# Output projection of a decoder layer: two column chunks at once, with two of eight row tile pairs by Strassen's scheme

## The chip, the core and the metric

One core of a Trainium2 chip runs one layer of a decoder trunk in float32. The metric is the device time in microseconds (us) of one execution. Engines: TensorE (PE) multiplies matrices into PSUM; VectorE (DVE) and ScalarE (ACT) work elementwise; GpSimd (POOL) does a little; SyncE (SP) issues nearly all transfers.

## The reference

The step around the change is the third line; all the others stay as they are.

```python
y_a = multiscale_pool(u_pool, pool_mix_w[i], pool_scale[i]) @ w_branch_a[i]
y_b = hgrn2(q, f_logit, inp, g, lb_all[i], hgrn_norm_w[i]) @ w_branch_b[i]
merged = jax.nn.sigmoid(gate_a) * y_a + jax.nn.sigmoid(gate_b) * y_b
x = x + merged @ w_out[i]                 # (256, 2048) @ (2048, 2048)
h2 = rms_norm(x, ln_ffn_w[i])
u = causal_depthwise_conv(h2 @ w_up[i], conv_w[i], conv_b[i])
```

There are 256 tokens and a model width of 2048.

## The kernel before

**Precision.** TensorE multiplies a shortened float32 form, so every operand is split into a high part and a remainder (hi and lo). One product of blocks is a triple of matmuls (`triple`, L717; the same in `row_tile`, L654): hi by hi, hi by lo, lo by hi. Each matmul has a 128x128 block of tokens as the stationary operand and 128x512 weights as the moving one.

**Units.** All weights are streamed through a ring of RING = 4 buffers. A unit is one transfer of two row tiles (2 x 128 rows) of 512 columns, 512 KB, into `raw`. ScalarE copies it to `w_hi` (`split_hi`, L1108), VectorE writes the remainder `w_lo` (`split_lo`, L1411), and TensorE multiplies it with the two row tiles of both token blocks: 2 x 2 triples, 12 matmuls (`unit`, L665). Units are numbered through the kernel: the mixer's gates and branches from MIX, the output projection from WOUT, the up projection from UP, the down projection from DOWN. A transfer into a buffer waits until the unit four before is split (`slot_split`, L481).

**Slots.** ScalarE and VectorE work through slots with a handwritten order, `slot(s)` (L1277 and L1756). Slot s first splits unit s + 3 (LEAD = 3); ScalarE's split waits until TensorE is through with unit s - 1, so slot s runs beside TensorE's unit s. Then follow the other steps that are due at s, in the order in which they stand in the code. An engine that waits holds all that stands behind it in its queue.

**The output projection before.** WOUT = UP - 32. Four column chunks of 512 one after the other, eight units each. `chunk_unit` (L698) waits for a free accumulator (`main`, one of two), multiplies, and runs what is due on TensorE behind the unit: `turn_m` (L709, turns the last merged chunk, behind unit 2) and `side` (L937). Chunk n ends at `out_slot(n)`. Then, for chunk n: VectorE adds the accumulator to x (L1838, two additions of 128x512, in slot out_slot(n)); TensorE turns x by eight transposes, `x1T` + n, behind unit out_slot(n) + 1, and waits for these additions before (L964); ScalarE squares x with a sum (L1166, slot + 1); ScalarE and VectorE write the high and low blocks of xT from the turned ones (L1143 and L1457, slot + 2). The up projection (L827) reads these blocks of xT; its first eight units are narrow (256 columns in all) and need a chunk of xT for every two of them.

**What already uses Strassen's scheme.** The gates of the mixer (chunks 1 to 3, both gates at a time, pairs GATES_AT = (2, 4)) and the down projection. For a pair of row tiles and two chunks, the 2 x 2 blocks of tokens and the 2 x 2 blocks of weights need 8 triples; the scheme needs 7, with sums of blocks. VectorE forms the differences of weights (`weight_diffs`, L1661) two slots ahead, ScalarE and VectorE split them in two halves (`sums_hi`, `sums_lo`); GpSimd and VectorE form the sums of the activations (`join_parts`, `act_sums`); TensorE does its part of them two units later (`gate_weight_sums`, L804). At the end the four products beside the accumulators are recombined by additions on VectorE (`combine_gates`, `combine`).

Of the kernel before, what the change touches and what calls it, by code (L numbers as in the profile page):

```python
# [36 lines left out]
P = 128  # L37
# [15 lines left out]
NCOL = 512  # L53
# [53 lines left out]

def out_slot(n):
    return WOUT + UK * (n + 1)
# [17 lines left out]
GATES_AT = (2, 4)  # L127
N_GATES = len(GATES_AT) * (NQ - 1)
SEVENS = [gate_unit(n, i) for n in range(1, NQ) for i in GATES_AT] + [down_unit(p, i) for p in range(2) for i in SEVEN_AT[p]]
SEVEN = {u: q for q, u in enumerate(SEVENS)}  # L130
ACT_SUMS = [0, 1] + SEVENS[N_GATES:]
SUMS_AT = {max(u - 4, DOWN + UK) if f > 1 else MIX + 2 * UK - 2 + 3 * f: f for f, u in enumerate(ACT_SUMS)}
N_SEVEN = [N_GATES + len(SEVEN_AT[0]), len(SEVENS)]
COMBINED0 = 4 * (NQ - 1)
# [67 lines left out]
GATES_COMBINE_AT = [gate_unit(n, GATES_AT[-1]) + 5 for n in range(NQ)]  # L202
COMBINE_AT = [down_slot(2 * p) - 4 for p in range(2)]
# [18 lines left out]
def build(nc, x, x_t, p_t, vecs, convs, w_in, pool_mix_w, w_branch_a, w_branch_b, w_out, w_up, w_down,  # L222
          w_ple_gate, w_ple, ln_final_w, ident_c, levels_c, counts_c, out):
    with ExitStack() as ctx:
# [255 lines left out]
        def _(sp):  # L480
# [70 lines left out]
            for n in range(NQ):  # L551
                for i in range(UK):
                    rows(u, w_out_v, 2 * i, n * NCOL)
                    x_tok_piece(u)
                    u += 1
# [46 lines left out]
        def _(pe):  # L602
# [123 lines left out]
            def act_sum(q, k):  # L726
                return a_sums_hi[:, q % 2, k, :], a_sums_lo[:, q % 2, k, :]
# [18 lines left out]
            def down_seven(u, p, i, a):  # L746

                q = SEVEN[u - a]
                first, end = i == SEVEN_AT[p][0], i == SEVEN_AT[p][-1]
                pe.wait_ge(lo_full, u + 1)  # L750
                if a == 0:
                    if first:
                        if p:
                            pe.wait_ge(xT_ready, 4 * (2 * NQ + 2))
                        else:
                            pe.wait_ge(z_read, NUP + 1)
                    triple(product(p, 0), *act_block(2 * i, 0), *ring_tile(u, 0), start=first, stop=end)
                    mm = triple(down_acc(2 * p, 0), *act_block(2 * i + 1, 0), *ring_tile(u, 1), start=False, stop=False)
                else:
                    pe.wait_ge(a_sums_ready, q + 3 - N_GATES)  # L760
                    mm = triple(down_acc(2 * p + 1, 0), *act_sum(q, 2), *ring_tile(u, 1), start=False, stop=False)
                mm.then_inc(units_done, 1)
# [26 lines left out]
            def gate_seven(u, n, i, a):  # L789

                q = SEVEN[u - a]
                first, end = i == GATES_AT[0], i == GATES_AT[-1]
                pe.wait_ge(lo_full, u + 1)
                if a == 0:
                    if first:
                        pe.wait_ge(gated, 4 * n)
                    triple(gate_product(0), *x_block_t(2 * i, 0), *ring_tile(u, 0), start=first, stop=end)
                    mm = triple(main[:, 0, 0, :], *x_block_t(2 * i + 1, 0), *ring_tile(u, 1), start=False, stop=False)
                else:
                    pe.wait_ge(a_sums_ready, q % 2 + 1)  # L800
                    mm = triple(main[:, 1, 0, :], *act_sum(q, 2), *ring_tile(u, 1), start=False, stop=False)
                mm.then_inc(units_done, 1)

            def gate_weight_sums(u, n, i, half):  # L804
# [9 lines left out]
                else:  # L814
                    triple(gate_product(2), *act_sum(q, 0), *sum_tile(q, 2), start=first, stop=end)
                    mm = triple(main[:, 0, 1, :], *x_block_t(2 * i + 1, 1), *sum_tile(q, 3), start=False, stop=False)
                mm.then_inc(w_sums_done, 1)
# [207 lines left out]
            for n in range(NQ):  # L1025
                for i in range(UK):
                    if n == 0 and i % 2 == 0:
# [79 lines left out]
        def _(ac):  # L1107
# [153 lines left out]
            def sums_hi(q, part):  # L1261

                if part == 0:
                    ac.wait_ge(a_summed, q + 1)
                    if q > 1:
                        ac.wait_ge(w_sums_done, 2 * (q + N_GATES - 3))
# [10 lines left out]
            def slot(s):  # L1277
# [23 lines left out]
                for p in range(2):  # L1301
                    if s == COMBINE_AT[p] - 1:
# [107 lines left out]
        def _(dve):  # L1410
# [317 lines left out]
            def combine(p, part):  # L1728

                c0, c1 = cols(2 * p), cols(2 * p + 1)  # L1730
                p5, p6, p7 = (product(p, k) for k in range(1, 4))
# [7 lines left out]
                if part == 0:  # L1739
                    dve.wait_ge(copied, NQ - 1 + p + 1)  # L1740
# [15 lines left out]
            def slot(s):  # L1756
# [20 lines left out]
                for p in range(2):  # L1777
                    if COMBINE_AT[p] <= s < COMBINE_AT[p] + 4:
# [33 lines left out]
                for n in range(NQ):  # L1812
# [132 lines left out]
        def _(pool):  # L1945
# [42 lines left out]
            def join_parts(f, u):  # L1988

                if f < 2:  # L1990
                    k, hi, lo = 2 * GATES_AT[f], xT_hi, xT_lo
                else:
                    k, hi, lo = u - DOWN - 2 * UD * (u >= DOWN + 2 * UD), aT_hi, aT_lo
                if f == 2:
# [14 lines left out]
            for f in range(2):  # L2009
                join_parts(f, 0)  # L2010
# [4 lines left out]
            for f, u in enumerate(ACT_SUMS[2:], 2):  # L2015
                join_parts(f, u)
# [51 lines left out]
```

## Time and profile before

| | us |
|---|---|
| median of 3 runs | 1432.1 (1432.09 to 1432.28) |
| the profiled execution | 1433.02 |
| its span | 1431.2 |

| engine | busy us | share of the span |
|---|---|---|
| TensorE | 1420.7 | 99% |
| VectorE | 1033.4 | 72% |
| ScalarE | 774.3 | 54% |
| GpSimd | 171.5 | 12% |

The mean granted clock of TensorE is 0.999 of full speed. The DMA engines move 191 GB/s on average. Matmuls are pipelined: one of 128x512 is shown with 0.39 us though the next starts 0.23 us later, so TensorE's work is counted by starts. The output projection lies between 521.96 and 612.57 us of the span.

### The profile page before, as it was taken

The page shows a single profiled execution, that of the slowest core. Times are in us where ns is not written, and L with a number is a line of the kernel's source. Part 1 is how long each engine was busy: PE and PEld are TensorE (multiplying, and loading weights), DVE is VectorE, ACT ScalarE, POOL GpSimd, SP SyncE. Part 2 cuts the span into 40 slices and gives each one's busy share as a digit, 9 for nine tenths or more (in the row PEclk, how much of TensorE's full clock was granted, in tenths as well). Part 3 has the DMA queues.
Part 4 walks back from the last instruction along what each step waited for, and adds up shares of the span by engine and source line. Part 5 has one row for each costly group of instructions (what it writes and reads, how often), then busy time and mean ns, then how long its engine had stood idle before and what let it go on. Part 6 is the DMA issues. An engine that isn't in the chain of part 4 may idle for free.

```text
span 1431.2 us, 19783 instructions
## 1 busy us (share of the span) xinstructions
PE 1420.7 (99%) x7094; PEld 1207.4 (84%) x7094; DVE 1033.4 (72%) x1284; ACT 774.3 (54%) x937; POOL 171.5 (12%) x115
## 2 busy tenths in 40 slices
PE   9999999999999999999999999999999999999997
PEld 7888888888888888888888888888888888888886
DVE  7676777867577765566777777777777888887755
ACT  7555655545454544455555555555555555555644
POOL 0044144100000000000111101111011110000000
PEclk9999999999999999999999999999999999999999
DMA  9655555455665665466656566565665555566663
GB/s 323 199 176 162 161 170 169 147 189 193 193 204 177 220 236 189 156 206 185 190 176 205 177 191 194 173 204 181 192 193 180 202 197 194 174 197 215 231 200 121
DMA packets 190876, 273.47 MB, mean 191 GB/s; under 512 B 11744, under 2 KB 103136, under 8 KB 190688
## 3 DMA queue, kind: packets, MB, share of 16 engines
q1 hardware_dynamic: 190384, 272.30, 59.4%
q8 instruction: 38, 0.62, 0.2%
q10 hardware_dynamic: 432, 0.37, 0.1%
q14 instruction: 22, 0.18, 0.0%
HBM read 270.53 MB, written 2.10 MB: 190 GB/s over the span
## 4 chain that ended last, share of the span: by engine, by line
PE 97%; DVE 1%; issue 0%; DMA 0%; ACT 0%; SPq 0%; ACTq 0%; POOLq 0%; POOL 0%; DVEq 0%
PE aux L839 11%; PE main L839 11%; PE main L661 10%; PE main L663 10%; PE main L662 10%; PE aux L848 6%; PE main L848 6%; PE main L719 5%; PE main L720 5%; PE main L721 5%; PE aux L719 3%; PE aux L720 3%; PE aux L721 3%; PE aux L662 2%; PE aux L661 2%; PE aux L663 2%
## 5 line engine op out<-in xcount | busy, mean ns | idle before, releaser
L1421 DVE TENSOR_TENSOR w_lo<-raw,w_hi 128x1024 fp32r<-128x1024 f32 (+1 forms) x484 | 596.8, 1244 | 337.8 <-ACT w_hi L1119 337.4
L1119 ACT ACTIVATE w_hi<-raw 128x1024 fp32r<-128x1024 f32 (+1 forms) x484 | 508.6, 1052 | 517.3 <-PE main L663 158.4
L661 PE MATMUL main<-w_hi,xT 128*128 128x512 f32 x510 | 201.4, 395 | 0.5 <-DVE w_lo L1883 0.3
L662 PE MATMUL main<-w_lo,xT 128*128 128x512 f32 x510 | 198.6, 389 | 0.0
L663 PE MATMUL main<-w_hi,xT 128*128 128x512 f32 x510 | 198.5, 389 | 0.0
L839 PE MATMUL aux<-xT,w_hi 128*128 128x512 f32 x704 | 169.8, 391 | 0.0
L839 PE MATMUL main<-xT,w_hi 128*128 128x512 f32 x672 | 163.0, 391 | 0.0
L839 PEld LDWEIGHTS aux<-xT,w_hi 128*128 128x128 f32 x704 | 129.3, 188 | 25.3 <-issue 0.3
L839 PEld LDWEIGHTS main<-xT,w_hi 128*128 128x128 f32 x672 | 123.2, 188 | 23.6
L2007 POOL TENSOR_TENSOR act<-cv 128x512 f32<-128x512 f32 (+1 forms) x22 | 71.9, 3267 | 418.8 <-DVE cv L1645 418.8
L661 PEld LDWEIGHTS main<-w_hi,xT 128*128 128x128 f32 x510 | 95.8, 188 | 20.3 <-DVE xT L1448 1.3
L663 PEld LDWEIGHTS main<-w_hi,xT 128*128 128x128 f32 x510 | 95.7, 188 | 20.0
L662 PEld LDWEIGHTS main<-w_lo,xT 128*128 128x128 f32 x510 | 95.9, 188 | 18.8
L848 PEld LDWEIGHTS aux<-xT,w_lo 128*128 128x128 f32 x704 | 90.3, 191 | 3.4
L848 PE MATMUL aux<-xT,w_lo 128*128 128x256 f32 x704 | 91.3, 283 | 0.0
L848 PEld LDWEIGHTS main<-xT,w_lo 128*128 128x128 f32 x672 | 86.4, 191 | 3.5
L848 PE MATMUL main<-xT,w_lo 128*128 128x256 f32 x672 | 87.5, 283 | 0.0
L1645 DVE SCALAR_TENSOR_TENSOR cv<-z,convT,cv 128x255 f32<-128x255 f32 (+1 forms) x172 | 71.7, 479 | 3.0
L1948 POOL TENSOR_TENSOR st<-st,minus_half 128x2 f32<-128x2 f32 (+1 forms) x5 | 3.2, 645 | 490.1 <-DVE st L1479 359.1
L719 PE MATMUL main<-w_hi,xT 128*128 128x512 f32 x150 | 58.6, 391 | 0.0
L721 PE MATMUL main<-w_hi,xT 128*128 128x512 f32 x150 | 58.4, 389 | 0.0
L720 PE MATMUL main<-w_lo,xT 128*128 128x512 f32 x150 | 58.4, 389 | 0.0
(305 smaller groups left out, 2115.3 us busy)
## 6 DMA issues: line engine op xcount, KB each, us to landing
raw<-in_w_up SPq DMA_DIRECT2D x336, 256.0 KB
raw<-in_w_in SPq DMA_DIRECT2D x136, 512.0 KB
raw<-in_w_down SPq DMA_DIRECT2D x84, 512.0 KB
raw<-in_w_out SPq DMA_DIRECT2D x32, 512.0 KB
raw<-in_w_ple_gate SPq DMA_DIRECT2D x32, 512.0 KB
raw<-in_w_branch_a SPq DMA_DIRECT2D x16, 512.0 KB
raw<-in_w_branch_b SPq DMA_DIRECT2D x16, 512.0 KB
raw<-in_w_in SPq DMA_DIRECT2D x15, 256.0 KB, 5.9
```

What stands on the lines that cost most here:

```text
L661: pe.matmul(acc, th, wh, start=first, stop=False)
L662: pe.matmul(acc, th, wl, start=False, stop=False)
L663: return pe.matmul(acc, tl, wh, start=False, stop=end)
L719: pe.matmul(acc, th, wh, start=start, stop=False)
L720: pe.matmul(acc, th, wl, start=False, stop=False)
L721: return pe.matmul(acc, tl, wh, start=False, stop=stop)
L839: mm = pe.matmul(up_acc(j, b), w_hi[:, u % RING, a, b * P:(b + 1) * P], xT[:, k, :, :].rearrange("p h t -> p (h t)"), start=(k == 0), stop ...
L848: mm = pe.matmul(up_acc(j, b)[:, 0:SEQ], w_lo[:, u % RING, a, b * P:(b + 1) * P], xT[:, k, 0, :], start=False, stop=False)
L1119: ac.activation(w_hi[:, u % RING, :, 0:w], raw[:, u % RING, :, 0:w], ACT.Copy).then_inc(hi_full, 1)
L1421: dve.tensor_tensor(w_lo[:, u % RING, :, 0:w], raw[:, u % RING, :, 0:w], w_hi[:, u % RING, :, 0:w].bitcast(F32), ALU.subtract).then_inc(lo ...
L1645: last_op = dve.scalar_tensor_tensor(out=cv[:, b, d:SEQ], in0=z[:, b, 0:SEQ - d], scalar=convT[:, tap, f0(f)], in1=cv[:, b, d:SEQ], op0=AL ...
L2007: pool.tensor_tensor(act[:, 0:nf, :], cv[:, 0:nf, :], cv[:, nf:2 * nf, :], ALU.mult).then_inc(prod_u, 1)
```

## The change

The four chunks of the output projection are taken as two pairs. In each pair the units go in the order OUT_ORDER: chunk a = 0 for row tile pairs 0 and 1, chunk a = 1 for them, then both chunks in turn for pairs 2 to 5, then chunk 0 for pairs 6 and 7 and chunk 1 for them. So the first chunk of a pair ends behind its 14th unit and the second behind its 16th. Row tile pairs 2 and 4 are done by Strassen's scheme, in the gates' manner: `out_seven` for the units themselves, `out_weight_sums` behind later units, with the gates' four places for the products (`gate_product`). The joined sums of m are formed once, in the last gate chunk, and serve both pairs. The products are recombined straight into x: eight additions on VectorE in two slots (`combine(..., out=True)`), the second of them the one in which the first chunk of the pair is added to x. The steps behind a chunk (L1838, x1T, squares, blocks of xT) keep their distances from out_slot.

```diff
+OUT_ORDER = ([(i, a) for a in range(2) for i in range(2)] + [(i, a) for i in range(2, UK - 2) for a in range(2)]
+             + [(i, a) for a in range(2) for i in range(UK - 2, UK)])
+def out_unit(p, i, a=0):
+    return WOUT + 2 * UK * p + OUT_ORDER.index((i, a))
 def out_slot(n):
-    return WOUT + UK * (n + 1)
+    return WOUT + 2 * UK * (n // 2) + 2 * UK - 2 + 2 * (n % 2)
...
+OUT_AT = ((2, 4), (2, 4))
...
+SUMS_AT.update((WOUT - 12 + 3 * f, len(GATES_AT) + f) for f in range(len(OUT_FORMS)))
...
+OUT_COMBINE_AT = [out_unit(p, OUT_AT[p][-1]) + 5 for p in range(2)]
...
-            for n in range(NQ):
-                for i in range(UK):
-                    rows(u, w_out_v, 2 * i, n * NCOL)
+            for p in range(2):
+                for i, a in OUT_ORDER:
+                    rows(u, w_out_v, 2 * i, (2 * p + a) * NCOL)
...
+            def out_seven(u, p, i, a):
+                q = SEVEN[u - a]
+                first, end = i == OUT_AT[p][0], i == OUT_AT[p][-1]
+                pe.wait_ge(lo_full, u + 1)
+                if a == 0:
+                    if first:
+                        if p:
+                            pe.wait_ge(xT_ready, 4 * (NQ + 2))
+                        else:
+                            pe.wait_ge(gated, 4 * NQ)
+                    triple(gate_product(0), *m_block_t(2 * i, 0), *ring_tile(u, 0), start=first, stop=end)
+                    mm = triple(main[:, 0, 0, :], *m_block_t(2 * i + 1, 0), *ring_tile(u, 1), start=False, stop=False)
+                else:
+                    pe.wait_ge(a_sums_ready, FORM[q] + 1)
+                    mm = triple(main[:, 1, 0, :], *act_sum(q, 2), *ring_tile(u, 1), start=False, stop=False)
+                mm.then_inc(units_done, 1)
+            def out_weight_sums(u, p, half):
...
+                pe.wait_ge(w_sums_ready, 2 * q + half + 1)
+                if half == 0:
+                    if first and p == 0:
+                        pe.wait_ge(mT_ready, NQ)
+                    triple(gate_product(1), *act_sum(q, 3), *sum_tile(q, 0), start=first, stop=end)
+                    mm = triple(gate_product(3), *act_sum(q, 1), *sum_tile(q, 1), start=first, stop=end)
+                else:
+                    triple(gate_product(2), *act_sum(q, 0), *sum_tile(q, 2), start=first, stop=end)
+                    mm = triple(main[:, 0, 1, :], *m_block_t(2 * i + 1, 1), *sum_tile(q, 3), start=False, stop=False)
...
-                    chunk_unit(u, C_WOUT + n, i, UK, mT_hi, mT_lo, 2 * i)
+                    if i == 0:
+                        main_released(C_WOUT + 2 * p + a - 2)
+                    if i in OUT_AT[p]:
+                        out_seven(u, p, i, a)
+                    else:
+                        unit(u, C_WOUT + 2 * p + a, i, UK, mT_hi, mT_lo, 2 * i)
+                    for half in range(2):
+                        if u - 2 - half in SEVEN:
+                            out_weight_sums(u - 2 - half, p, half)
+                    for name in AUX_AT.get(u, ()):
+                        side(name)
...
+                    if s == OUT_COMBINE_AT[p] - 1:
+                        done = 2 * (N_GATES + sum(map(len, OUT_AT[:p + 1])))
+                        ac.wait_ge(w_sums_done, done)
+                        ac.wait_ge(w_sums_ready, done)
+                        ac.activation(w_sums[:, 0, :], gate_product(0), ACT.Copy).then_inc(copied, 1)
...
+                    if OUT_COMBINE_AT[p] <= s < OUT_COMBINE_AT[p] + 2:
+                        for part in range(2):
+                            combine(p, 2 * (s - OUT_COMBINE_AT[p]) + part, out=True)
...
-                            if norm == 1 and n == 0:
-                                dve.wait_ge(tok_in, 16 * NQ)
-                            if norm == 2:
-                                dve.wait_ge(combined, combines[0])
+                            dve.wait_ge(combined, combines[0])
```

## Rows read from the trace of the kernel before

**Rows 1.** The page: busy time of the engines, and the chain that ended last.
```profile
PE 1420.7 (99%) x7094; PEld 1207.4 (84%) x7094; DVE 1033.4 (72%) x1284; ACT 774.3 (54%) x937; POOL 171.5 (12%) x115
...
PE 97%; DVE 1%; issue 0%; DMA 0%; ACT 0%; SPq 0%; ACTq 0%; POOLq 0%; POOL 0%; DVEq 0%
```

**Rows 2.** Waits of TensorE, first and last of six: us in total, times, longest.
```profile
PE main L972 <- DVE junk L1876: 1.1, 1, 1.1
...
PE main L719 <- DVE w_lo L1421: 0.2, 1, 0.2
```

**Rows 3.** Stretches: start:end length, busy us (instructions) per engine, clock, DMA share, GB/s.
```profile
457.14:500.20 43.06, 43.06 (x196) 35.74 (x194) 33.64 (x34) 21.45 (x22) 0.00 (x0) 1.00 0.62 208
...
521.96:612.57 90.61, 90.61 (x417) 75.38 (x416) 49.40 (x54) 41.93 (x57) 0.00 (x0) 1.00 0.51 169
```

**Rows 4.** TensorE in order of time: start, duration, instruction, operands.
```profile
468.92 0.39 PE L719 MATMUL aux<-w_hi,xT 128*128 128x512 f32 x1
...
521.96 0.39 PE L661 MATMUL main<-w_hi,mT_hi 128*128 128x512 f32 x1
...
530.12 1.03 PE L714 MATMUL aux<-ident,m_tok 128*128 128x128 f32 x8
...
531.23 0.40 PE L662 MATMUL main<-w_lo,mT_hi 128*128 128x512 f32 x1
...
615.13 0.40 PE L839 MATMUL main<-xT,w_hi 128*128 128x512 f32 x1
615.55 1.06 PE L880 MATMUL aux<-ident,x_tok 128*128 128x128 f32 x8
```

**Rows 5.** VectorE in order of time, last gate chunk: differences of weights, recombination.
```profile
464.12 1.22 DVE L1666 TENSOR_TENSOR w_sums<-raw 128x1024 f32<-128x1024 f32 x1
...
466.71 1.22 DVE L1421 TENSOR_TENSOR w_lo<-raw,w_hi 128x1024 fp32r<-128x1024 f32 x1
...
494.53 0.68 DVE L1703 TENSOR_TENSOR sig_b<-aux,w_sums 128x512 f32<-128x512 f32 x1
495.25 0.69 DVE L1703 TENSOR_TENSOR w_sums<-aux,sig_b 128x512 f32<-128x512 f32 x1
```

**Rows 6.** VectorE in order of time, output projection and start of the up projection.
```profile
523.31 1.23 DVE L1421 TENSOR_TENSOR w_lo<-raw,w_hi 128x1024 fp32r<-128x1024 f32 x1 [1.49 <-ACT w_hi L1119]
...
547.10 1.28 DVE L1838 TENSOR_TENSOR x_tok<-main,x_tok 128x512 f32<-128x512 f32 x2
...
551.40 1.23 DVE L1421 TENSOR_TENSOR w_lo<-raw,w_hi 128x1024 fp32r<-128x1024 f32 x1 [1.50 <-ACT w_hi L1119]
552.55 1.65 DVE L1457 SCALAR_TENSOR_TENSOR xT<-aux,vecT,xT 128x256 fp32r<-128x256 f32 x4
...
605.33 0.69 DVE L1421 TENSOR_TENSOR w_lo<-raw,w_hi 128x512 fp32r<-128x512 f32 x1 [1.06 <-ACT w_hi L1119]
...
614.12 1.28 DVE L1838 TENSOR_TENSOR x_tok<-main,x_tok 128x512 f32<-128x512 f32 x2
```

**Rows 7.** ScalarE in order of time, output projection and start of the up projection.
```profile
550.32 1.06 ACT L1119 ACTIVATE w_hi<-raw 128x1024 fp32r<-128x1024 f32 x1 [0.30 <-PE main L663]
...
604.67 0.63 ACT L1119 ACTIVATE w_hi<-raw 128x512 fp32r<-128x512 f32 x1 [1.66 <-PE main L663]
...
615.44 0.63 ACT L1166 ACTIVATE junk<-x_tok 128x512 f32<-128x512 f32 x1 [0.60 <-DVE x_tok L1838]
...
616.83 0.62 ACT L1119 ACTIVATE w_hi<-raw 128x512 fp32r<-128x512 f32 x1
617.35 1.55 ACT L1143 ACTIVATE xT<-aux,vecT 128x256 fp32r<-128x256 f32 x4
```

**Rows 8.** TensorE's last matmul, and stretches behind it (the eighth figure is the clock).
```profile
1422.86 0.28 PE L1102 MATMUL main<-w_hi,pT_lo 128*128 128x256 f32 x1
...
1427.00:1428.00 1.00, 0.00 (x0) 0.00 (x0) 0.42 (x1) 0.61 (x1) 0.00 (x0) 1.00 0.37 143
1428.00:1429.00 1.00, 0.00 (x0) 0.00 (x0) 0.00 (x0) 0.00 (x0) 0.00 (x0) 0.50 1.05 404
```

More of the change, by code:

```diff
@@ L127 @@
 GATES_AT = (2, 4)
+OUT_AT = ((2, 4), (2, 4))
 N_GATES = len(GATES_AT) * (NQ - 1)
-SEVENS = [gate_unit(n, i) for n in range(1, NQ) for i in GATES_AT] + [down_unit(p, i) for p in range(2) for i in SEVEN_AT[p]]
+N_OUTS = sum(map(len, OUT_AT))
+SEVENS = ([gate_unit(n, i) for n in range(1, NQ) for i in GATES_AT] + [out_unit(p, i) for p in range(2) for i in OUT_AT[p]]
+          + [down_unit(p, i) for p in range(2) for i in SEVEN_AT[p]])
 SEVEN = {u: q for q, u in enumerate(SEVENS)}
[L131 to L134, printed above, removed]
+OUT_FORMS = sorted(set(OUT_AT[0] + OUT_AT[1]))
+DOWN_FORMS = len(GATES_AT) + len(OUT_FORMS)
+FORM = ([f for n in range(1, NQ) for f in range(len(GATES_AT))] + [len(GATES_AT) + OUT_FORMS.index(i) for p in range(2) for i in OUT_AT[p]]
+        + [DOWN_FORMS + q for q in range(len(SEVENS) - N_GATES - N_OUTS)])
+N_FORMS = FORM[-1] + 1
+SUMS_AT = {MIX + 2 * UK - 2 + 3 * f: f for f in range(len(GATES_AT))}
+SUMS_AT.update((WOUT - 12 + 3 * f, len(GATES_AT) + f) for f in range(len(OUT_FORMS)))
+SUMS_AT.update((max(u - 4, DOWN + UK), FORM[q]) for u, q in SEVEN.items() if u >= DOWN)
+N_SEVEN = [N_GATES + N_OUTS + len(SEVEN_AT[0]), len(SEVENS)]
+COMBINED_OUT = 4 * (NQ - 1)
+COMBINED0 = COMBINED_OUT + 16
 def gate_slot(n):
@@ L726, in act_sum @@
             def act_sum(q, k):
-                return a_sums_hi[:, q % 2, k, :], a_sums_lo[:, q % 2, k, :]
+                return a_sums_hi[:, FORM[q] % 2, k, :], a_sums_lo[:, FORM[q] % 2, k, :]
             def ring_tile(u, t):
@@ L799, in gate_seven @@
                 else:
-                    pe.wait_ge(a_sums_ready, q % 2 + 1)
+                    pe.wait_ge(a_sums_ready, FORM[q] + 1)
                     mm = triple(main[:, 1, 0, :], *act_sum(q, 2), *ring_tile(u, 1), start=False, stop=False)
@@ L1024, in _ @@
                         u += 1
-            for n in range(NQ):
-                for i in range(UK):
-                    if n == 0 and i % 2 == 0:
+            for p in range(2):
+                for i, a in OUT_ORDER:
+                    if p == 0 and a == 0 and i % 2 == 0:
                         pe.wait_ge(mT_ready, i // 2 + 1)
-                    chunk_unit(u, C_WOUT + n, i, UK, mT_hi, mT_lo, 2 * i)
+                    if i == 0:
[9 more added lines that the diff above has]
+                        side(name)
+                    if u in MT_AT:
+                        turn_m(MT_AT[u])
                     u += 1
@@ L1265, in sums_hi @@
                     if q > 1:
-                        ac.wait_ge(w_sums_done, 2 * (q + N_GATES - 3))
+                        ac.wait_ge(w_sums_done, 2 * max(r + 1 for r in range(len(SEVENS)) if FORM[r] == q - 2))
                     ac.activation(a_sums_hi[:, q % 2].rearrange("p k t -> p (k t)"), a_sums[:].rearrange("p k t -> p (k t)"),
@@ L1726, in sum_gates, with combine @@
                     dve.tensor_tensor((sig_a, sig_b)[k][:, tb, :], main[:, k, tb, :], t[2 * tb + k], ALU.add).then_inc(gate_sums, 1)
-            def combine(p, part):
+            def combine(p, part, out=False):
                 c0, c1 = cols(2 * p), cols(2 * p + 1)
-                p5, p6, p7 = (product(p, k) for k in range(1, 4))
+                p5, p6, p7 = (gate_product(k) if out else product(p, k) for k in range(1, 4))
                 t = [w_sums[:, k, :] for k in range(4)]
@@ L1739, in combine @@
                 if part == 0:
-                    dve.wait_ge(copied, NQ - 1 + p + 1)
+                    if out and p == 0:
+                        dve.wait_ge(tok_in, 16 * NQ)
+                    dve.wait_ge(copied, NQ - 1 + p + 1 + (0 if out else 2))
                     add(x_tok[:, 0, c0], t[0], x_tok[:, 0, c0])
@@ L2007, in product @@
                 pool.tensor_tensor(act[:, 0:nf, :], cv[:, 0:nf, :], cv[:, nf:2 * nf, :], ALU.mult).then_inc(prod_u, 1)
-            for f in range(2):
-                join_parts(f, 0)
+            for f in range(DOWN_FORMS):
+                join_parts(f)
             root(1)
@@ L2014, in _ @@
                 product(1, 2, it)
-            for f, u in enumerate(ACT_SUMS[2:], 2):
-                join_parts(f, u)
+            for f in range(DOWN_FORMS, N_FORMS):
+                join_parts(f)
             root(2)
```

18 lines of the change are left out of this document (14 added, 4 removed).

## The prediction

> **What bounds the kernel now.** I read the page first: TensorE is busy for 1420.7 of 1431.2 us, and 97% of the chain that ended last lies on it [rows 1]. Its waits come next: six rows of one wait each for the whole kernel, from 1.1 us, at the very start, down to 0.2 us [rows 2]. The stretches follow: in the output projection, 521.96 to 612.57, TensorE is busy in all 90.61 us, while VectorE is busy for 49.40 and ScalarE for 41.93; in the gate stage before it, which already has paired chunks with Strassen's scheme at pairs 2 and 4, TensorE is busy in all of 43.06 us and VectorE for 33.64 [rows 3]. So TensorE's own instructions set the time, the other two engines have slack on average, and the question is whether they have it at each place where TensorE will wait for them.
>
> The measure of TensorE is the distance of two starts, not the shown duration: from 521.96 to 530.12 stand 36 matmuls (units 0 to 2), so one costs 0.2267 us and a plain unit of twelve 2.72 us. Eight transposes delay the next units by 0.9 us: 1.11 from their start to the second matmul behind them, less one matmul [rows 4].
>
> I count units of this stage from 0 (the line name WOUT) to 31; unit 32 is the first of the up projection.
>
> **What is saved.** A Strassen pair of row tiles needs 7 triples of matmuls where two plain units need 8: 21 for 24. Two pairs in each of two chunk pairs: 12 matmuls, 12 x 0.2267 = 2.72 us. Transposes, transfers and bytes stay as they are. With 1432.1 us, 2.72 us is 0.19%.
>
> **What is added and lies beside TensorE.** For each Strassen pair, ScalarE's two 128x1024 copies and VectorE's differences and two 128x1024 remainders; two more joins of the m tiles with their sums, at slots 12 and 15 of the last gate chunk. The gate stage runs this with the same spacing (Strassen units 4, 5, 8 and 9 behind the turn of m at unit 2) and TensorE is without a gap there [rows 3], and of the kernel's six waits none behind the start is over 0.3 us [rows 2]. I take these at nothing for the first chunk pair: VectorE's 9.4 idle us of that stretch (43.06 - 33.64) hide them; without these each us that VectorE comes late is one of TensorE's. No transfer is moved past another: SyncE's order of transfers changes only in which weight columns they bring.
>
> **What is moved.** Before, a chunk ends every eight units, and its steps (x added, x turned, squares, the high and low blocks of xT) have eight units to go through. Now chunks 0 and 1 end behind units 13 and 15, chunks 2 and 3 behind 29 and 31, and eight additions of the recombination stand on VectorE in front of the first of each two. They are put in two slots (13 and 14; 29 and 30), four in each. TensorE's turn of a chunk waits for x, two units behind the chunk's end. I follow VectorE by starts, times relative to the start of unit 13.
>
> Durations: VectorE begins a slot's split 1.35 us behind the unit's start, 521.96 to 523.31 [rows 4, 6]; from a split to what follows 1.15, 551.40 to 552.55; two independent 128x512 additions are 0.60 apart (1.28 for both, 0.68 for one); the last ends 0.68 behind its start [rows 5, 6]; an addition that waits for the one before starts 0.72 behind it, 494.53 to 495.25 [rows 5]; TensorE's first transpose stands 0.15 behind the end of the x additions (614.12 + 1.28 to 615.55) [rows 4, 6].
>
> *Hole 1, the turn of chunk 0 behind unit 15.* Split at 1.35; additions at 2.50, 3.10, 3.82, 4.42 (the third waits); split of slot 14 at 5.02; additions at 6.17, 6.77, 7.49, 8.09 (the seventh waits); x of chunk 0 at 8.81 (it waits) and 9.41; end 10.09; transposes at 10.24. TensorE is ready at 3 x 2.72 = 8.16. It stands for 2.08 us.
>
> *Hole 2, the turn of chunk 1 behind unit 17.* ScalarE squares x from 10.13, takes 1.39 (615.44 to 616.83), then splits; VectorE's split starts 1.08 behind that (550.32 to 551.40) [rows 6, 7], at 12.60; the low blocks of chunk 0 at 13.75 take 1.65, of which the next start hides 0.08; x of chunk 1 at 15.32 and 15.92; end 16.60; transposes 16.75. TensorE is ready at 10.24 + 0.9 + 5.44 = 16.58: 0.17 us.
>
> *Hole 3, unit 20, the first Strassen unit of the second pair, waits for the low blocks of chunk 1.* Squares from 16.64 to 18.03; the half split on VectorE 0.67 later (as 604.67 to 605.33, [rows 6, 7]) at 18.70; the differences for unit 20 stand in the queue in front of the low blocks: at 19.31, for 2.59 (464.12 to 466.71) [rows 5]; low blocks 21.90 to 23.55; TensorE at 23.70 instead of 16.75 + 0.9 + 5.44 = 23.09: 0.61 us.
>
> Then 90 matmuls, 20.40 us, to unit 28. The differences for unit 20 end 1.8 us ahead of it, those for the gates' unit 4 ended 2.2 ahead (466.71 against 468.92 [rows 4, 5]); I count no further wait.
>
> *Hole 4, the turn of chunk 2 behind unit 31.* As hole 1, but the splits are those of the narrow up units: the first begins 0.92 behind the start of unit 29 (605.33 [rows 6]; that unit started at 612.57 - 3 x 2.72) and costs 0.60, having the shape of an addition. 0.92 + 0.60 + 1.92 + 0.60 + 0.60 + 1.92 + 0.72 + 0.60 + 0.68 + 0.15 = 8.71 against 8.16: 0.55 us.
>
> *Hole 5, the turn of chunk 3 behind unit 33.* Before, chunk 2 was long done here, and TensorE waited 0.19 us (615.13 + 0.23 to 615.55 [rows 4]). Now from the end of x of chunk 2: squares 0.04 + 1.39, narrow split 0.66 later on VectorE, another 0.68 until two of ScalarE's four high blocks are there (0.52 + 1.55 / 2 from its split, 616.83 to 617.35 [rows 7], and 0.04), low blocks 1.57, x of chunk 3 0.60 + 0.68, and 0.15: 5.77. TensorE has 0.15 + 0.9 + 2.79 (two narrow units, 612.57 to 615.36) = 3.84. Hole 1.93, 1.74 more than before. What follows hangs on x of chunk 3 as before and moves with it.
>
> **Sum.** 2.08 + 0.17 + 0.61 + 0.55 + 1.74 = 5.15 us of holes, less 2.72 us of matmuls: +2.4 us. The profiled execution took 1433.0 us (span 1431.2 and 1.8 around it), 0.9 above the median; it would become 1435.4, and the median 1432.1 becomes **1434.5 us**. Each hole is a difference of two chains of about eight us, and I allow 0.2 us for each; all of one sign make 1 us.
>
> The trace of before shows no such hole of TensorE; whether its restart costs more than the 0.15 us is bounded by the rows that are nearest: 0.15 at 615.55, and the 0.3 us of the waits [rows 2]. Five holes with 0.15 more would add 0.75. I take 0.15, the same kind of step, and keep the rest in the range.
>
> A rule against the 0.72: additions that wait for each other start 0.12 us later than those that don't [rows 5, 6]. The Trainium skill, VectorE: DVE Perf Modes, section "The DRAIN you can't avoid", says that a semaphore behind each operation costs nothing extra, since the next one waits for the pipeline anyway. By that, three waits each in holes 1 and 4 would be free, 6 x 0.12 = 0.72 us, and the result 1433.8; the rows show the 0.12, and I go by them.
>
> **Rivals.**
> *No holes.* VectorE's chain is shorter than I read it, or the transposes find x in time: then all 2.72 us arrive, 1429.4 us. For it: VectorE is idle for 41 us of the 90 [rows 3]. Against it: it is the order of four additions per slot that counts, 3.67 us with the split, for a unit of 2.72. Chance 0.09. More than 2.72 + 0.19 us cannot be gained here.
> *The transfer for unit 24 comes late.* Its ring buffer is free only when the differences for unit 20 are done, at 21.9; TensorE wants unit 26 split at 35.9, and between stand the split of 24, a remainder, the half split, the differences for 24 and the split of 26, about 1.14 + 1.14 + 0.6 + 2.6 + 1.14, and ScalarE's copy, 1.1: 7.7 us. The transfer may so take 6.3 us. In the gate stage no TensorE wait came of it; beyond that point each us of transfer is a us of TensorE. With 2 us: 1436.5. Chance 0.15, any further VectorE lateness in the second pair included.
> *The clock falls in holes 1 and 5.* The granted clock is at its upper level in all of this stage; behind the last matmul (1422.86 + 0.28) it was still there between 1427 and 1428 and at half in 1428 to 1429 [rows 8], after some 4.9 us of rest. Holes 1 and 5 with their transposes are some 2.9 us without matmuls. If they sufficed, and the lower level (1.2 GHz for 2.4) lasted as long as such a hole, each would cost about half of it in addition and the first matmuls run at twice their time: 2 x 1.5 = 3 us, 1437.5, slower. It decides from the length of rest at which the clock gives way, which the rows put at 4.9 us there. Chance 0.08. The Trainium skill, TensorE: Matmul & The Clock Gate, section "Why this matters for your kernels", advises against idle gaps between bursts of matmuls for this reason; [rows 8] agree that it falls, though not within 2.9 us.
>
> **How the numbers follow.** The likeliest, 0.68: holes as computed, 1434.5, from 1433.5 to 1435.6. 0.2% of 1432.1, what a measurement of this kernel can tell, is 2.9 us: the limits are 1429.2 and 1435.0. About 0.28 of the likeliest case lies above 1435.0: 0.19; with 0.14 of the transfer and 0.08 of the clock, slower has 0.41. Faster than 1429.2 needs all of the saving and the old 0.19 us too: 0.02. The rest, 0.57, is within. The range leaves out most of the first and the clock's rival: 1432.6 to 1437.0.
>
> **What would show it.** 12 fewer matmuls of 128x512 in the stage; waits of TensorE on the x additions of about 2.1 us (once at transposes behind unit 15), 0.2, 0.5 and 1.9, and one of 0.6 on low blocks of xT; in the first Strassen group no wait at all. If the waits on x are missing, my VectorE chain is wrong; if the matmuls near a hole lie 0.45 us apart, it was the clock; if TensorE waits for w_lo around units 24 to 27, it was the transfer.

## The result and the profile after

The changed kernel took 1435.8 us (median of 13 runs, 1435.2 to 1436.7) against 1432.4 us for the kernel before beside it (13 runs, 1432.1 to 1433.5): a ratio of 1.0023, 95% interval 1.0016 to 1.0031. It is slower by 3.4 us, where 1434.5 was forecast from 1432.1 (+2.4). The profiled execution took 1435.77 us, its span is 1434.0 us.

The page of the changed kernel, the lines that answer to [rows 1]:

```profile
PE 1419.4 (99%) x7082; PEld 1206.1 (84%) x7082; DVE 1062.6 (74%) x1330; ACT 782.2 (55%) x949; POOL 174.2 (12%) x117
...
PE 96%; DVE 2%; issue 1%; ACT 0%; DMA 0%; ACTq 0%; POOLq 0%; POOL 0%; DVEq 0%
```

The twelve matmuls are gone (7082 for 7094), VectorE has 29 us more work, and its share of the chain that ended last rose from 1% to 2%. TensorE's waits, the first row, which has no like in [rows 2] (in us in total, times, longest):

```profile
PE aux L937 <- DVE x_tok L1914: 4.3, 3, 2.0
```

Line numbers are those of the changed kernel from here on: L937 are the transposes of x (L880 before), L1914 the additions to x (L1838), L1811 the recombination, L1495 VectorE's part of the weights' split (L1421), L1531 the low blocks of xT (L1457), L682 to L684 the three matmuls of a product.

VectorE in order of time at the first chunk pair's end, which answers to [rows 5, 6]:

```profile
557.90 1.23 DVE L1495 TENSOR_TENSOR w_lo<-raw,w_hi 128x1024 fp32r<-128x1024 f32 x1 [2.58 <-ACT w_hi L1188]
559.05 0.68 DVE L1811 TENSOR_TENSOR x_tok<-w_sums,x_tok 128x512 f32<-128x512 f32 x1
559.65 2.01 DVE L1811 TENSOR_TENSOR w_sums<-aux,w_sums 128x512 f32<-128x512 f32 x3
561.57 1.22 DVE L1495 TENSOR_TENSOR w_lo<-raw,w_hi 128x1024 fp32r<-128x1024 f32 x1
562.70 0.68 DVE L1811 TENSOR_TENSOR w_sums<-aux,w_sums 128x512 f32<-128x512 f32 x1
563.30 2.01 DVE L1811 TENSOR_TENSOR x_tok<-x_tok,w_sums 128x512 f32<-128x512 f32 x3
565.42 1.29 DVE L1914 TENSOR_TENSOR x_tok<-main,x_tok 128x512 f32<-128x512 f32 x2
```

These are two slots of a split and four additions each, and x of chunk 0 behind them: 3.67 us from the first split to the second, and 3.85 us from there to x. TensorE beside it (the bracket gives the idle time before, and what ended it):

```profile
564.49 0.39 PE L684 MATMUL main<-w_hi,mT_lo 128*128 128x512 f32 x1
566.86 1.52 PE L937 MATMUL aux<-ident,x_tok 128*128 128x128 f32 x8 [1.98 <-DVE x_tok L1914]
568.03 0.77 PE L682 MATMUL main<-w_hi,mT_hi 128*128 128x512 f32 x1
568.60 0.63 PE L683 MATMUL main<-w_lo,mT_hi 128*128 128x512 f32 x1
569.03 0.63 PE L684 MATMUL main<-w_hi,mT_lo 128*128 128x512 f32 x1
...
571.20 0.40 PE L684 MATMUL main<-w_hi,mT_lo 128*128 128x512 f32 x1
```

This is hole 1, the time without a start beyond the 0.2267 us that one matmul takes: 564.49 + 0.2267 to 566.86, 2.14 us. Behind it the matmuls start 0.43 us apart instead of 0.23. The stretches there, as in [rows 8] (the clock is the figure before the last two):

```profile
567.00:568.00 1.00, 1.00 (x8) 1.00 (x8) 0.84 (x1) 0.97 (x3) 0.00 (x0) 0.65 0.00 0
568.00:569.00 1.00, 1.00 (x4) 0.84 (x3) 0.00 (x0) 1.00 (x3) 0.00 (x0) 0.50 0.07 14
...
571.00:572.00 1.00, 1.00 (x6) 0.82 (x5) 1.00 (x4) 0.00 (x0) 0.00 (x0) 1.00 0.34 100
```

The granted clock fell to its lower level (1.2 GHz for 2.4) while the transposes behind hole 1 ran; in the stretch from 571 it is back at the upper one. The end of the second chunk pair, TensorE again, answers to the last rows of [rows 4]:

```profile
612.27 0.39 PE L684 MATMUL main<-w_hi,mT_lo 128*128 128x512 f32 x1
613.14 1.06 PE L937 MATMUL aux<-ident,x_tok 128*128 128x128 f32 x8 [0.48 <-DVE x_tok L1914]
...
615.90 1.09 PE L896 MATMUL main<-xT,w_hi 128*128 128x512 f32 x4
618.78 1.06 PE L937 MATMUL aux<-ident,x_tok 128*128 128x128 f32 x8 [1.78 <-DVE x_tok L1914]
```

Holes 4 and 5: 0.64 us (612.27 + 0.23 to 613.14), and 1.97 us where before had 0.21 by the same count of starts.

To compare kernels I use one length: from the first matmul of the output projection to the first of the second up tile (`aux<-xT,w_hi`). It holds the whole change and none of the scatter of the rest. Before: 521.96 to 625.13, 103.17 us. The changed kernel: 521.66 to 628.37, 106.71 us, so +3.54 lie in it, 0.18 from the +3.36 of the medians. I call it *the length* below.

### The profile page after: what moved, and what is told of

It reads as the page before. It is cut to its first block, busy times and chain, and to the rows that moved or that the text cites. A ratio compares the mean times of both kernels' runs of the same rounds, so it can differ in the third digit from the quotient of the medians.

```text
span 1434.0 us, 19847 instructions
## 1 busy us (share of the span) xinstructions
PE 1419.4 (99%) x7082; PEld 1206.1 (84%) x7082; DVE 1062.6 (74%) x1330; ACT 782.2 (55%) x949; POOL 174.2 (12%) x117
## 4 chain that ended last, share of the span: by engine, by line
PE 96%; DVE 2%; issue 1%; ACT 0%; DMA 0%; ACTq 0%; POOLq 0%; POOL 0%; DVEq 0%
PE aux L896 11%; PE main L896 11%; PE main L682 9%; PE main L684 9%; PE main L683 9%; PE aux L905 6%; PE main L905 6%; PE main L740 5%; PE main L742 5%; PE main L741 5%; PE aux L740 3%; PE aux L742 3%; PE aux L741 3%; PE aux L682 2%; PE aux L684 2%; PE aux L683 2%
## 5 line engine op out<-in xcount | busy, mean ns | idle before, releaser
L1495 DVE TENSOR_TENSOR w_lo<-raw,w_hi 128x1024 fp32r<-128x1024 f32 (+1 forms) x480 | 592.0, 1245 | 308.9 <-ACT w_hi L1188 308.2
L682 PE MATMUL main<-w_hi,xT 128*128 128x512 f32 x510 | 201.4, 395 | 0.3 <-DVE w_lo L1959 0.3
L684 PE MATMUL main<-w_hi,xT 128*128 128x512 f32 x510 | 198.5, 389 | 0.0
L682 PEld LDWEIGHTS main<-w_hi,xT 128*128 128x128 f32 x510 | 95.8, 188 | 20.0 <-DVE xT L1522 1.0
L684 PEld LDWEIGHTS main<-w_hi,xT 128*128 128x128 f32 x510 | 95.7, 188 | 20.0
L1319 ACT ACTIVATE cv<-z,convT 128x256 f32<-128x256 f32 x86 | 44.8, 591 | 24.0 <-DVE z L1710 24.0
```

The costliest lines, as they stand in the source:

```text
L682: pe.matmul(acc, th, wh, start=first, stop=False)
L684: return pe.matmul(acc, tl, wh, start=False, stop=end)
L1495: dve.tensor_tensor(w_lo[:, u % RING, :, 0:w], raw[:, u % RING, :, 0:w], w_hi[:, u % RING, :, 0:w].bitcast(F32), ALU.subtract).then_inc(lo ...
```

## The experiments

The theory: VectorE's order makes five holes of TensorE, which cost more than the twelve matmuls save; in hole 1 the clock fell in addition. The rivals: VectorE's sheer amount of work; the new order of chunks alone; the clock as the main loss; something late behind these.

**The additions left out.** `combine` returns after its waits where it stands for the output projection, so x lacks these parts; the count of additions that later waits rely on is lowered by sixteen:

```diff
                     dve.wait_ge(copied, NQ - 1 + p + 1 + (0 if out else 2))
+                if out:
+                    return
+                if part == 0:
```

> Leaves out the sixteen additions that recombine the products of the output projection (eight for each chunk pair); x so lacks these parts. All else, the moved chunk ends among it, stays. Theory (VectorE's additions stand in front of the x additions and so make holes 1 and 4 and a part of hole 5, and the clock falls because of hole 1): TensorE waits for x only in the up projection's second unit, about 0.85 us; no fall of the clock; 1432.4 - 2.72 + 0.66 = 1430.3 us. Rival (it is the two-unit distance of the chunk ends, with squares, turns and blocks of xT, that TensorE waits for): the holes stay nearly as they are, 1434.5 to 1435.8.

Measured: 1431.2 us (11 runs), ratio 0.9992 (0.9983 to 1.0001); the length is 101.53 us, 1.64 less than before. Holes 1 to 4 are gone. One wait on x is left, the last turn:

```profile
614.04 1.06 PE L937 MATMUL aux<-ident,x_tok 128*128 128x128 f32 x8 [1.11 <-DVE x_tok L1917]
```

It is a hole of 1.29 us by starts, not the 0.85 that I expected. 2.72 - (1.29 - 0.21) = 1.64: the length adds up to within 0.01 us. So the whole saving does arrive; the sixteen additions cost 4.3 us of length (105.87, from a trace of the changed kernel in which the clock stays up, shown further down, less 101.53); and part of hole 5 has nothing to do with them.

**The new order alone, without Strassen's scheme.**

```diff
-OUT_AT = ((2, 4), (2, 4))
+OUT_AT = ((), ())
```

with the recombination and its waits taken out accordingly.

> The new order of the output projection (two column chunks at once, twice) with no scheme of Strassen: 12 matmuls more than the changed kernel, no recombination additions. Theory: the order alone brings hole 5, 1.1 to 1.3 us where it was 0.19 before, and no other hole and no fall of the clock, so 1432.42 + 0.9 to 1.1 = 1433.3 to 1433.5 us; and 12 matmuls of 0.2267 us are all that it is longer by than the kernel without the additions, so 1431.23 + 2.72 = 1433.95 us by that way. Rival: the order costs nothing, hole 5 comes from Strassen's second pair alone: 1432.4 us, and the last turn is late by 0.2 us as before.

Measured: 1433.5 us (11 runs), ratio 1.0007 (0.9998 to 1.0016); the length is 104.23 us, +1.06. The same hole, and no other:

```profile
616.61 1.06 PE L937 MATMUL aux<-ident,x_tok 128*128 128x128 f32 x8 [1.10 <-DVE x_tok L1916]
```

1.29 - 0.21 = 1.08: the order of the chunks alone costs this. The rival that it costs nothing is out. Against the kernel without additions it is 104.23 - 101.53 = 2.70 us longer, the twelve matmuls (2.72), and that again is what was saved.

**The additions one slot earlier.** ScalarE's copy of the first product moves with them:

```diff
-OUT_COMBINE_AT = [out_unit(p, OUT_AT[p][-1]) + 5 for p in range(2)]
+OUT_COMBINE_AT = [out_unit(p, OUT_AT[p][-1]) + 4 for p in range(2)]
...
-                    if s == OUT_COMBINE_AT[p] - 1:
+                    if s == OUT_COMBINE_AT[p]:
```

> VectorE makes the eight additions of each pair one slot earlier (slots 12 and 13, 28 and 29). Theory: x of the first chunk is then ready 0.6 us (pair 1) and 2 us (pair 2) ahead of TensorE; holes 1, 2 and 4 go and with hole 1 the fall of the clock; hole 3 is 0.2 us, hole 5 1.2 us: 1432.4 - 2.72 + 0.24 + 0.99 = 1430.9 us. Rival (the additions then wait for the last products and hold up the splits behind them): TensorE waits for w_lo around units 14 to 16, 1433 or more.

Measured: 1431.3 us (11 runs), ratio 0.9993 (0.9984 to 1.0002); the length is 101.77 us. VectorE in order of time:

```profile
558.99 0.68 DVE L1811 TENSOR_TENSOR w_sums<-aux,w_sums 128x512 f32<-128x512 f32 x1
559.59 2.01 DVE L1811 TENSOR_TENSOR x_tok<-x_tok,w_sums 128x512 f32<-128x512 f32 x3
561.52 1.22 DVE L1495 TENSOR_TENSOR w_lo<-raw,w_hi 128x1024 fp32r<-128x1024 f32 x1
562.66 1.28 DVE L1914 TENSOR_TENSOR x_tok<-main,x_tok 128x512 f32<-128x512 f32 x2
```

The same sixteen additions are done, with x ready at 563.94 for transposes at 564.66. Of the five holes, 1, 2 and 4 are gone, 3 is 0.16 us, and 5 is 1.29, as with the order alone. Against the kernel without additions the length is 0.24 us longer, where the changed kernel's is 4.3 us longer. So it is not the amount of VectorE's work that costs, but that the additions stand directly in front of the x that TensorE turns next.

**x of the second chunk first.** In the slots in which the low blocks of a pair's first chunk stood ahead of x of its second, the two change places (`x_add` is the loop of L1914 as a function; at its old place it is left out for these two chunks):

```diff
+                for n in (1, 3):
+                    if s == out_slot(n):
+                        x_add(C_WOUT + n, n, 1)
                 for n in range(NQ):
                     for k, sig in ((2, sig_a), (3, sig_b)):
...
```

> In slots 16 and 32 VectorE adds x of the pair's second chunk before it writes the low blocks of the first, instead of behind. Theory: hole 5 shrinks from 1.97 to 0.3 us, holes 1 and 4 and the fall of the clock stay: 1435.8 - 1.7 = 1434.1 us. Rival (the low blocks, now later, hold up TensorE in turn at the up projection's fifth unit): no gain, 1435.8.

Measured: 1434.1 us (10 runs; seven at 1433.3 to 1434.2, three at 1435.7 to 1438.2), ratio 1.0016 (1.0007 to 1.0026). Hole 1 is unchanged (2.13), hole 5 is down to 0.27 us: that was the low blocks in front of x. Hole 3 is gone too, since x of chunk 1, with which its chain begins, is earlier: from the turn of chunk 1 to that of chunk 2 this trace has 38.25 us, 0.71 less than the changed kernel with the clock up. Two lines were not expected. The clock stayed up behind the same hole 1, and a new wait, 1.04 us by starts, stands at the second up tile:

```profile
568.00:569.00 1.00, 1.00 (x6) 0.82 (x5) 0.00 (x0) 1.00 (x3) 0.00 (x0) 1.00 0.10 20
```

```profile
625.97 1.40 PE L896 MATMUL aux<-xT,w_hi 128*128 128x512 f32 x5 [0.86 <-DVE rB L1951]
```

rB holds the norm's factors; VectorE copies them out of the memory that the second up tile's products go to. Followed back, this copy stands in VectorE's queue behind the splits of two up units, and ScalarE's parts of both had waited for their transfers (ScalarE, then SyncE):

```profile
621.77 1.06 ACT L1188 ACTIVATE w_hi<-raw 128x1024 fp32r<-128x1024 f32 x1 [1.75 <-DMA raw<-in_w_up]
623.17 1.06 ACT L1188 ACTIVATE w_hi<-raw 128x1024 fp32r<-128x1024 f32 x1 [0.34 <-DMA raw<-in_w_up]
```

```profile
617.48 0.37 SPq L523 DMA_DIRECT2D raw<-in_w_up  x1
618.40 1.44 SPq L523 DMA_DIRECT2D raw<-in_w_up  x1
```

Transfers are issued and copied in the order of the units. The issue of 1.44 us, where 0.37 is usual, brings the second of these two units and accounts for at most the 0.34 us that its copy waited. The longer wait, 1.75 us, is for the first unit. Its transfer was issued at 617.48 in the usual time, and by the landings in the trace its last part came 4.27 us later, where in the trace of before and in that of both moves, below, the same unit's took 3.42. Why it took longer is not shown.

**Both moves together.**

> The two moves of the earlier experiments together: the recombination additions one slot earlier, and x of a pair's second chunk added ahead of the low blocks of its first. If the changed kernel loses by the order on VectorE alone, holes 1 to 4 are gone or under 0.2 us and hole 5 is down from 1.29 us (additions earlier alone) to about 0.27 us (x first alone), so 1431.33 - 1.02 = 1430.3 us. Rival: the copy of rB is next late, as in the profiled execution with x first, where the first unit of the second up tile waited 1.04 us for it behind a weight transfer whose issue took 1.44 us: then 1431.3 us, with a wait on rB of 0.8 us or more. If that wait was one slow issue of that execution, the trace shows no wait on rB.

Measured: 1430.4 us (11 runs, 1429.6 to 1430.7; before beside it 1432.35), ratio 0.9985 (0.9976 to 0.9994): shorter than the kernel before, by 0.15%, and than either move alone. The length is 100.47 us, 2.70 less than before: the whole saving (the 0.21 us that before had at the last turn are gone too, and about as much is new at the second up tile). TensorE at the last turn and at the second up tile:

```profile
612.53 1.04 PE L937 MATMUL aux<-ident,x_tok 128*128 128x128 f32 x8
...
622.32 2.08 PE L896 MATMUL aux<-xT,w_hi 128*128 128x512 f32 x8
```

No wait on x is left in the stage. At the second up tile a gap of 0.32 us is left where the changed kernel has 0.06 to 0.09: rB is indeed the next thing late, by a little. The 1.04 us of the trace with x first do not come back in this one. The medians give 2.0 us of the 2.70; the other 0.7 is within the interval.

**Hole 1 filled.** Nine matmuls with a block of zeros stand in front of the last product of unit 15, so that TensorE doesn't rest; they add nothing to the sum (ScalarE writes the block long before):

```diff
+                        if u == WOUT + 15 and a == 1 and tb == 1:
+                            pe.wait_ge(zero_set, 1)
+                            for _ in range(ZEROS):
+                                pe.matmul(main_acc(c, tb, width), zero[:], w_hi[:, u % RING, a, 0:width], start=False, stop=False)
```

> Nine matmuls with a stationary block of zeros (2.04 us) are put into unit 15, so that TensorE works through hole 1 instead of resting; VectorE's chain is untouched. Theory (the fall of the clock behind hole 1 costs about 1.6 us by itself, and hides 0.8 us of holes 2 and 3): the clock keeps its upper level throughout the stage, small waits come back behind unit 17 (0.17) and at unit 20 (0.6), about 1434.9 us, and the runs scatter less. Rival 1 (the fall costs nothing, since the time would be lost in holes 2 and 3 anyway): 1435.8. Rival 2 (without the fall all of 1.6 us comes back): 1434.2.

Measured: 1435.3 us (11 runs), ratio 1.0019 (1.0010 to 1.0028); the length is 105.84 us, 0.87 less than that of the changed kernel's profiled execution. The clock stays at 1.00. Hole 3, which that execution did not show, is there, TensorE at unit 20:

```profile
580.60 0.47 PE L747 MATMUL aux<-w_hi,mT_hi 128*128 128x512 f32 x1 [0.38 <-DVE xT L1541]
```

So the slow matmuls cost more than 0.87 us, and gave back holes 2 and 3: TensorE was late enough to find their data ready. By the times, 1435.3 against 1435.8, the two can't be told apart; the trace tells them apart.

**The changed kernel again, unaltered, for its trace.** Three more:

> The changed kernel once more, unaltered, for its trace: whether the granted clock falls behind hole 1 in every execution. If the hole of 2.14 us followed by eight transposes is always enough, 0.50 stands in the stretch from 1 to 3 us after the hole's end, and the time is 1435.2 to 1436.7 us. If it falls in some executions alone, as with x first, where the same hole of 2.13 us left it at 1.00, this trace or the next has 1.00 there, holes 2 and 3 of 0.1 and 0.5 us are back, and the span is some 0.8 us shorter than 1434.0 us.

> As the run before it: the changed kernel unaltered, a further trace of the clock behind hole 1, with the same two expectations (0.50 there in every execution and a span of about 1434.0 us, or 1.00 in some, with holes 2 and 3 back and about 1433.2 us).

> The changed kernel unaltered, for a fourth trace of the clock behind hole 1: so far 0.50 in one of three, the stretch being 106.71 us with it and 105.87 and 105.88 us without. One of these two again; a value between them, or above 106.71, would show a fall of another length.

Measured: 1435.6, 1435.0 and 1436.3 us; the length is 105.88, 105.87 and 105.85. In none of the three did the clock fall behind hole 1, which has 2.14 to 2.15 us in each. The second of them, TensorE and the stretch behind the hole:

```profile
567.05 1.06 PE L937 MATMUL aux<-ident,x_tok 128*128 128x128 f32 x8 [1.98 <-DVE x_tok L1914]
...
580.46 0.47 PE L740 MATMUL aux<-w_hi,mT_hi 128*128 128x512 f32 x1 [0.38 <-DVE xT L1531]
```

```profile
568.00:569.00 1.00, 1.00 (x7) 0.83 (x6) 0.03 (x1) 1.00 (x3) 0.00 (x0) 1.00 0.00 0
```

So of four traces of one and the same kernel, one has the fall.

**Hole 1 made longer.** Three additions of 128x312 into a scratch tile, each waiting for the one before, ahead of x of chunk 0:

```diff
+                            if norm == 1 and n == 0:
+                                for r in range(LAGS):
+                                    if r:
+                                        dve.wait_ge(lag, r)
+                                    dve.tensor_tensor(fill[:], main_acc(c, 0)[:, 0:FILL], x_tok[:, 0, 0:FILL], ALU.add).then_inc(lag, 1)
+                                dve.wait_ge(lag, LAGS)
```

> Three additions of 128x312 into a scratch tile, each waiting for the one before, ahead of x of chunk 0 on VectorE: by the 0.60 us of two additions of 128x512 and the 0.12 us of a wait, 0.49 us each, so hole 1 grows from 2.14 to about 3.6 us and nothing else changes. If the length of the rest decides whether the granted clock falls, 0.50 stands behind hole 1 in every trace of this kernel, and the stretch from the first matmul of the output projection to the first of the second up tile is 105.88 + 1.45 + 0.84 = 108.2 us (106.71 in the execution of the changed kernel where it fell, 105.88 and 105.87 where not). If the fall doesn't depend on the length (another cause, by chance in one execution of three), 1.00 stands there in most traces, and the stretch is 107.3 us. The time 1437.0 to 1438.0 us by the first, about 1437.0 by the second.

> The kernel with the longer hole once more, for a second trace: 0.50 behind hole 1 again and a stretch of 108.2 us if the length of the rest decides, 1.00 and 107.3 us in some if it doesn't.

Measured: 1437.6 us (5 runs: 1437.0, 1437.4, 1437.6, 1439.4, 1440.0), ratio 1.0042 (1.0028 to 1.0057), and 1438.8 us for the single run of the second. Hole 1 has 3.68 us in both traces. The first trace, and then the second:

```profile
567.00:568.00 1.00, 0.00 (x0) 0.00 (x0) 0.97 (x3) 0.00 (x0) 0.00 (x0) 1.00 0.00 0
568.00:569.00 1.00, 0.50 (x5) 0.53 (x6) 1.00 (x2) 0.61 (x2) 0.00 (x0) 1.00 0.00 0
```

```profile
567.00:568.00 1.00, 0.00 (x0) 0.00 (x0) 0.97 (x3) 0.00 (x0) 0.00 (x0) 0.56 0.00 0
568.00:569.00 1.00, 0.47 (x3) 0.50 (x4) 1.00 (x2) 0.58 (x2) 0.00 (x0) 0.50 0.00 0
```

The same rest, at the same place to 0.03 us, with the clock up in one and down in the other. The lengths are 107.39 and 109.16 us: here the fall costs 1.77. In the second the clock fell while TensorE still rested (0.56 in the stretch without a matmul), ahead of the transposes. The length of the rest alone doesn't decide, or the first trace would have 0.50 too. That it falls by chance is borne out, and the length of 107.3 us expected with the clock up was met; the price of a fall put at 0.84 us was too low. The granted clock that each run lists, a mean over the execution, is 0.998 in the three shorter of the five runs, 0.996 in the two longest and 0.995 in the second kernel's run, whose trace has the fall: probably three of the six had one.

**The kernel before again, for what lies outside the length.**

> The kernel before once more, for a second trace: what lies outside the stretch from the first matmul of the output projection to the first of the second up tile. Before's span less this stretch was 1431.2 - 103.17 = 1328.0 us, that of seven of the kernels with the change 1327.2 to 1328.2 us. If the change costs nothing outside, this one lies in 1327.2 to 1328.2 us again, with 103.17 us for the stretch; if it does, before is at 1326.9 us or less and its 1328.0 was an exception.

Measured: 1432.5 us, span 1430.7, length 103.16 us. Outside it lie 1327.5 us here and 1328.0 in the first trace; in the four traces of the changed kernel 1327.3, 1327.9, 1327.3 and 1328.6. No cost of the change outside the length is to be seen; single executions scatter there by a microsecond.

## Why the prediction was right where it was right, and wrong where it was wrong

The length in legs between the turns of x, from the starts of the eight transposes, in us. The kernel with both moves has no hole up to the last turn, so its legs serve as zero; "hole" is the changed kernel, with the clock up, less that.

| leg, up to | changed, clock fell | changed, clock up | both moves | hole | forecast |
|---|---|---|---|---|---|
| turn of chunk 0 | 45.20 | 45.20 | 43.06 | 2.14 | hole 1: 2.08 |
| turn of chunk 1 | 8.01 | 6.49 | 6.33 | 0.16 | hole 2: 0.17 |
| turn of chunk 2 | 38.27 | 38.96 | 37.62 | 1.34 | holes 3 and 4: 1.16 |
| turn of chunk 3 | 5.64 | 5.65 | 3.67 | 1.98 | hole 5: 1.93 |
| second up tile | 9.59 | 9.58 | 9.79 | | |
| the length | 106.71 | 105.88 | 100.47 | | |

- **What is saved, right.** 2.72 us forecast; 2.70 between the kernel with the order alone and that without additions, 2.70 between before and the kernel with both moves.
- **First Strassen group at nothing, right.** No wait of TensorE there in any trace.
- **The holes, right, together a little small.** The chain of hole 1 came out step by step: split, additions and x of chunk 0 were forecast at 1.35, 2.50, 3.10, 5.02, 6.17 and 8.81 behind the start of unit 13, and with that unit's start at 564.49 + 0.23 - 8.16 = 556.56 the rows have 1.34, 2.49, 3.09, 5.01, 6.14 and 8.86. Over all legs the holes are 0.28 us larger than forecast (0.06, -0.01, 0.18 and 0.05), so that the length grows by 2.71 instead of 2.43 us with the clock up. The largest term, 0.18, belongs to holes 3 and 4; hole 4 alone has 0.64 by starts for 0.55.
- **Hole 5, right in its size and in its cause.** The order of the chunks alone makes 1.29 us of it (the turn of chunk 3 follows that of chunk 2 by two narrow units, and the low blocks stand between), the late additions the rest; with x ahead of the low blocks 0.27 us are left, and with both moves nothing.
- **The rule on the semaphore.** By the Trainium skill, VectorE: DVE Perf Modes, section "The DRAIN you can't avoid", as I read it, six waits would have cost nothing, and the forecast would have been 1433.8. The trace agrees as to the semaphore that an addition raises: each of them raises one, and those that wait for none are still 0.60 us apart. It disagrees as to the wait for the addition just before: the three additions from 563.30, one of which waits so, show 2.01 us, where 0.60 + 0.60 + 0.68 would make 1.88, and x behind them, which waits too, starts at 565.42, 0.11 after their end, where in the kernel with earlier additions the split, which waits for none of them, starts 0.08 before it.
- **The transfer for unit 24, rightly a rival only.** No wait for w_lo appears around units 24 to 27.
- **The clock, the step that failed.** I let it decide "from the length of rest at which the clock gives way, which the rows put at 4.9 us". [rows 8] show one rest, at the kernel's end, and bound nothing from below: the clock fell behind 2.14 us of rest in one trace of four, and within a rest of 3.68 in one of two. The price per hole, about 1.5 us, was right for hole 1 (8.01 - 6.49 = 1.52), but it isn't a loss in full: late matmuls find what they would have waited for, and the next leg is 0.69 shorter, so 0.83 us remain. Behind hole 5 it fell in no trace, though that is nearly as long. At the kernel's end itself the 14 traces of this case have the fall anywhere from 1.9 to 5.0 us behind the last matmul; 4.9 was one draw. The shortest (x first) and the longest (the changed kernel), each with the last matmul and the stretch in which the clock fell:

```profile
1423.18 0.28 PE L1171 MATMUL main<-w_hi,pT_lo 128*128 128x256 f32 x1
1425.00:1426.00 1.00, 0.00 (x0) 0.00 (x0) 0.16 (x1) 0.08 (x1) 0.56 (x1) 0.67 1.04 426
```

```profile
1425.61 0.28 PE L1171 MATMUL main<-w_hi,pT_lo 128*128 128x256 f32 x1
1430.00:1431.00 1.00, 0.00 (x0) 0.00 (x0) 0.17 (x1) 0.36 (x1) 0.00 (x0) 0.94 0.63 244
```

The median of +3.4 us lies between +2.71, the length with the clock up, and +3.54, with it down. What share of the 13 runs had a fall isn't known; with one in four it would be 2.71 + 0.83 / 4 = 2.9. The 0.5 us that are then left are within the interval of the ratio (+2.3 to +4.4 us).

The granted clock that each run lists narrows this. No execution whose trace has a fall behind hole 1 lists 0.999. Five of the 13 runs do, so very likely they had none: 1435.2 to 1435.6 us, median 1435.4, which is +3.0. The other eight list 0.998 or 0.997 and take 1435.6 to 1436.7 us, median 1436.1; among 61 runs of the kernel before, those with 0.998 are no longer than those with 0.999 (a median of 1432.4 us for both). So more than one run in four may have had a fall, but a trace without one lists 0.998 too, and the share stays open, as do the 0.3 us between +2.71 and +3.0.

The forecast of 1434.5 stood on the right mechanism and was 0.96 us too low by the difference of the medians: 0.28 from the holes' sizes, some tenths (at most 0.83) from the clock, the rest unexplained. The sign was put as "within 0.2%" with 0.57 and slower with 0.41; it came out at 0.23%, just beyond that line of 2.9 us, from which the forecast of +2.4 was 0.5 us away; the interval, 0.16% to 0.31%, holds the line.

## What to carry to other kernels

An engine with 40 idle microseconds in a stage can still be what its neighbour waits for: count its queue slot by slot ahead of each result that somebody waits for, by starts, and put work that nobody waits for behind that result or a slot earlier. Here the same sixteen additions cost 4.3 us of length or 0.24, by one slot's difference; an exchange of two lines took off another 1.3. And a hole of the busiest engine is priced with the clock that may fall behind it, as a chance and not as a threshold, less the waits that the delay then hides.

## What was not expected of the hardware

- **The clock after the same rest.** Behind hole 1 of 2.13 to 2.15 us, with eight transposes between it and the next matmul, the granted clock fell in one of five traces (four of the changed kernel, one with x first), and with a rest of 3.68 us in one of two. In the first of these falls the clock went down during the transposes, in the second before them; behind hole 5, nearly as long and with transposes too, it never did. The cost to the next turn was 1.52 and 2.45 us. The Trainium skill, TensorE: Matmul & The Clock Gate, section "What's actually happening", says that the chip judges activity on a time base that runs on freely, whatever the kernel does; by that, equal rests would be treated unequally from execution to execution. The traces agree with that, and show no more of its cause.
- **Slow issues.** Of SyncE's 715 issues in an execution, between one and five take 0.8 to 1.8 us in each of the 14 traces, where the median is 0.39. None is shown to have cost TensorE much: the one of 1.44 us with x first at most 0.34 us, and one of 1.54 us at 619.23 in the first repeat of the changed kernel nothing: its length of 105.88 us is that of the other two repeats (105.87 and 105.85).
